# Second block, layer 0: seven half-size products for four projection pairs and three output pairs

## What is computed

```python
def second_block(x, c, ctx, c_ctx, w_mod, b_mod, ..., w_in, ..., w_out, ...):
    z = ctx
    for l in range(DEPTH):                                        # DEPTH = 2
        ...                                                       # first feed-forward part
        hx = modulate(rms_norm_2(x), mx[3], mx[4]) @ w_in[l]      # 1024 -> D_IN columns
        hz = modulate(rms_norm_2(z), mz[3], mz[4]) @ w_in[l]
        mix_x, mix_z = token_mixing(hx, hz, ...)                  # fourier, neighbourhood attention,
                                                                  # gated linear attention, grouped attention
        x = x + mx[5] * (mix_x @ w_out[l])                        # 1024 -> 1024
        ...                                                       # second feed-forward part
        if not last:
            z = z + mz[5] * (mix_z @ w_out[l])
```

## Time and profile before

| | us |
|---|---|
| median of 3 runs | 3211.98 |
| all runs | 3211.64, 3211.98, 3214.20 |
| the profiled execution | 3210.66 |
| its span in the trace | 3208.9 |
| projection stage, first plain tile (1708.03) to the product after it (1779.74) | 71.7 |
| output stage, end of the last transposes (1934.12) to the sums of the next norm (1984.36) | 50.2 |

### The profile page before, as it was taken

How to read it: one execution, slowest core, us unless ns; L and a number is a source line. 1 busy time by engine, 2 the same in 40 slices (tenths; PEclk the granted TensorE clock), 3 DMA queues, 4 the chain that set the end, 5 groups by cost and what they waited for, 6 DMA issues and landing times.

```text
span 3208.9 us, 45998 instructions
## 1 busy us (share of the span) xinstructions
PE 3165.5 (99%) x17760; PEld 2696.8 (84%) x17760; DVE 2046.9 (64%) x3824; ACT 770.5 (24%) x1786; POOL 123.7 (4%) x221
## 2 busy tenths in 40 slices
PE   8999999999999999999999989999999999999999
PEld 7888899988888999888885645888888888866999
DVE  6678668666785586786863773564445646356575
ACT  2121124221211242210114362211122111145221
POOL 0000000000000000100000000000000000001000
PEclk9999999999999999999999999999999999999999
DMA  6744675556446665564534122652325535232563
GB/s 192 190 112 150 218 217 159 170 159 158 114 155 203 171 173 166 151 189 136 174 130 118 35 51 73 170 184 79 102 72 162 185 119 156 87 106 54 145 176 128
DMA packets 587609, 456.26 MB, mean 142 GB/s; under 512 B 27792, under 2 KB 568880, under 8 KB 587008
## 3 DMA queue, kind: packets, MB, share of 16 engines
q1 hardware_dynamic: 564544, 373.65, 40.5%
q0 software_dynamic: 21376, 77.97, 7.7%
q10 hardware_dynamic: 1472, 1.68, 0.2%
HBM read 452.21 MB, written 1.05 MB: 141 GB/s over the span
## 4 chain that ended last, share of the span: by engine, by line
PE 94%; DVE 2%; ACT 1%; POOL 1%; issue 1%; DMA 1%; ACTq 0%; DVEq 0%; SPq 0%
PE psum L2552 53%; PE psum L2338 31%; PE psum L2345 3%; PE psum L2768 3%; PE psum L2744 1%; PE psum L2703 0%; ACT arena L1598 0%; PE psum L2641 0%; POOL hh L1360 0%; PE psum L2413 0%; DVE arena L1996 0%; POOL arena L1247 0%; PE psum L2579 0%; PE psum L2376 0%; PE psum L2562 0%
## 5 line engine op out<-in xcount | busy, mean ns | idle before, releaser
L2338 PE MATMUL psum<-hh,ring 128*128 128x256 f32 (+1 forms) x3584 | 855.5, 397 | 3.3 <-DVE hh L1841 3.0
L2338 PEld LDWEIGHTS psum<-hh,ring 128*128 128x128 f32 x3584 | 677.4, 191 | 153.5 <-issue 69.3
L2552 PE MATMUL psum<-arena 128*128 128x128 f32 (+1 forms) x4288 | 728.5, 327 | 2.8 <-ACT arena L1620 2.0
L2552 PEld LDWEIGHTS psum<-arena 128*128 128x128 f32 x4288 | 651.3, 191 | 59.0 <-issue 3.8
L1620 ACT ACTIVATE arena<-psum 128x256 f32<-128x256 f32 (+1 forms) x608 | 207.4, 341 | 1115.6 <-PE psum L2552 1113.7
L2552 PE MATMUL psum<-arena,ring 128*128 128x256 f32 (+1 forms) x2544 | 449.6, 329 | 2.4 <-ACT arena L1620 2.4
L2552 PEld LDWEIGHTS psum<-arena,ring 128*128 128x128 f32 x2544 | 393.8, 191 | 37.7 <-issue 3.7
L2552 PE MATMUL psum<-hh,ring 128*128 128x256 f32 (+1 forms) x1920 | 349.9, 335 | 3.8 <-ACT hh L1607 3.8
L2552 PEld LDWEIGHTS psum<-hh,ring 128*128 128x128 f32 x1920 | 302.1, 192 | 38.0 <-issue 5.9
L2552 PE MATMUL psum<-hh,arena 128*128 128x256 f32 (+1 forms) x1664 | 329.3, 341 | 0.0
L2105 DVE TENSOR_TENSOR arena<-arena 128x256 f32<-128x256 f32 (+1 forms) x168 | 61.1, 364 | 382.3 <-ACT arena L1620 380.3
(11 more groups left out here) (291 smaller groups left out, 2428.6 us busy)
## 6 DMA issues: line engine op xcount, KB each, us to landing
ring<-in_ffn_w SPq DMA_DIRECT2D x176, 512.0 KB, 5.2
ring<-in_w_in SPq DMA_DIRECT2D x54, 1024.0 KB, 5.3
ring<-in_w_up SPq DMA_DIRECT2D x88, 512.0 KB, 5.2
ring<-in_w_in SPq DMA_DIRECT2D x84, 512.0 KB, 5.3
mod_rows<-in_w_mod_rows POOLq DMA_DIRECT2D x72, 512.0 KB, 3.8
mod_rows<-in_w_mod_late_rows POOLq DMA_DIRECT2D x60, 512.0 KB, 4.7
ring<-in_ffn_w SPq DMA_DIRECT2D x16, 1536.0 KB, 6.6
ring<-in_ffn_w SPq DMA_DIRECT2D x16, 1280.0 KB, 5.8
```

Source lines behind the costliest of these rows:

```text
L2338: ins = mm(o[0:rows_, 0:T], w[:, k, c0:c0 + rows_], src[:, k, 0:T], start=(k == 0), stop=(k == kt - 1))
L2552: ins = mm(o, lhs[q][:, k, :], src[q][:, k, :], start=(q not in HALF_AFTER and not second and k == 0), stop=(k == n - 1), skip_group_check ...
```

## The change

In layer 0 of the second block only:

- **Projection.** `gate_in`, tile `np` 0 and the two gates stay plain and first. The eight other tiles become four pairs by seven products, in the order gq (gqa_q), naq (na_q), nak (na_k), glaqk (gla_q and gla_k). VectorE makes the activations' sums (`hsum2`, four instructions) and the weights' sums of each pair. ScalarE copies product 0 of a pair (`pair_copy`), then does the squares and the last copy of the pair before (`pair_out`), then the pair's other copies. `nss` and `nrot` of a pair stand one pair later.
- **Output.** `out_front` 2 is gone, tiles 0 and 1 stay plain, tiles 2 to 7 become three pairs by seven products. `hsum3` (six VectorE instructions) makes the sums of the mixed activations after the last `at_o`.
- Chunks are loaded in the new order: gk, gq, naq, nak, glaqk.

```diff
@@ plan_second
+    def seven(key, *ahead):
+        p.step("pair_copy", l, key)
+        for k in ahead:
+            p.step("pair_out", l, k)
+        p.half_part(("pair", l, PAIR, key), HALF_ORDER)
...
+    else:
+        p.step("hsum2", l)
+        p.step("wsum", l, PAIR, "pair", "gq")
+        project_plain(0)
+        gates()
+        p.step("wsum", l, PAIR, "pair", "naq")
+        seven("gq")
+        squared(0)
+        p.step("wsum", l, PAIR, "pair", "nak")
+        seven("naq", "gq")
+        squared(1)
+        squared(2)
+        turned(0)
+        p.step("wsum", l, PAIR, "pair", "glaqk")
+        seven("nak", "naq")
...
+        seven("glaqk", "nak")
+        squared(5)
+        squared(6)
+        turned(2)
+        p.step("pair_out", l, "glaqk")
...
-        if n == len(units) + 1:
+        if n == len(units) + 1 and last:
             out_front(2)
...
+        if not last and i == 0:
+            p.step("hsum3", l)
+        if not last and i in (0, 2, 4):
+            p.step("wsum", l, OUT, "pair", OUT_PAIRS[i // 2])
+        if not last and i // 2 in OUT_PAIRS:
+            if i % 2 == 0:
+                p.half_part(("pair", l, OUT, i // 2), HALF_ORDER)
+            continue
         p.step("out", l, i)
@@ ScalarE
+                elif kind == "pair_copy":
+                    name = ("pair", l, PAIR, r[0])
...
+                    produced(act, j)
+                    do(nc.scalar.activation(copy_of(name, 0), half_bank(name, 0), ACT.Copy), half_copied,
+                       4 * n + half_copies(name).index(0) + 1)
+                elif kind == "pair_out":
...
+                    evacuated(act, job[(*name, 5)])
...
+                        do(nc.scalar.activation(sqb2[:, 1, :], lead_of(name), ACT.Square), pair_squared, 2 * m + 1)
...
+                    free(nc.scalar.activation(val_of(name)[:, 0:S], bank(j)[:, 0:S], ACT.Copy), j)
...
+                        do(nc.scalar.activation(sqb2[:, 0, :], val_of(name), ACT.Square), pair_squared, 2 * m + 2)
@@ VectorE
+                elif kind == "hsum2":
...
+                    do(tt(p_t1, b12, b11, ALU.subtract))
...
+                    do(tt(p_t4, b21, p_t2, ALU.subtract), pair_summed, 1)
+                elif kind == "hsum3":
...
+                    for m in range(n_units // 2):
+                        evacuated(dve, job[("at_o", l, m)])
...
+                    do(tt(o_t4, mixt[:, 4:KT, 0:S], o_t2, ALU.subtract), pair_summed, 2)
@@ TensorE
+                        if kind == "pair" and q in (2, 4):
+                            pe.wait_ge(pair_summed, 1 + (w == OUT))
```

More of the change, by code:

```diff
@@ L55 @@
 HALF = S // 2
-FIRST = 2
+FIRST, PAIR, OUT = 2, 3, 4
+PAIR_KEYS = ("gq", "naq", "nak", "glaqk")
+OUT_PAIRS = (1, 2, 3)
 UP_SUMS = (3, 7, 11, 15, 19, 21)
@@ L552, in plan_second, with project_plain @@
     chunk_of = {6: "gk", 4: "gq", 5: "gq", 0: "naq", 1: "naq", 2: "nak", 3: "nak"}
-    for n in range(len(order) + 2):
-        if n < len(order):
-            p.step("np", l, n, order[n])
-            p.job("np", l, n, chunk=("w2", l, chunk_of[order[n]]))
-        if n == 0:
-            for d in range(2):
-                p.step("gate", l, d)
-                p.job("gate", l, d)
-            for i in range(2):
-                p.step("gp", l, i)
-                p.job("gp", l, i, chunk=("w2", l, "glaqk"))
-        if 1 <= n <= len(order):
-            p.step("nss", l, n - 1, order[n - 1])
-            p.job("nss", l, n - 1)
-        m = n - 3 if last else n - 2
-        if m >= 0 and order[m] >= 4:
-            p.step("nrot", l, m, order[m])
-            p.job("nrot", l, m)
+    def project_plain(n):
+        p.step("np", l, n, order[n])
+        p.job("np", l, n, chunk=("w2", l, chunk_of[order[n]]))
@@ new lines, in gates, with squared, turned @@
+    def gates():
+        for d in range(2):
+            p.step("gate", l, d)
+            p.job("gate", l, d)
+    def squared(n):
+        p.step("nss", l, n, order[n])
+        p.job("nss", l, n)
+    def turned(n):
+        p.step("nrot", l, n, order[n])
+        p.job("nrot", l, n)
+    def seven(key, *ahead):
[3 more added lines that the diff above has]
+        p.half_part(("pair", l, PAIR, key), HALF_ORDER)
+    if last:
+        for n in range(len(order) + 2):
+            if n < len(order):
+                project_plain(n)
+            if n == 0:
+                gates()
+                for i in range(2):
+                    p.step("gp", l, i)
+                    p.job("gp", l, i, chunk=("w2", l, "glaqk"))
+            if 1 <= n <= len(order):
+                squared(n - 1)
+            m = n - 3
+            if m >= 0 and order[m] >= 4:
+                turned(m)
+    else:
+        p.step("hsum2", l)
+        p.step("wsum", l, PAIR, "pair", "gq")
+        project_plain(0)
+        gates()
+        p.step("wsum", l, PAIR, "pair", "naq")
[8 more added lines that the diff above has]
+        seven("nak", "naq")
+        squared(3)
+        squared(4)
+        turned(1)
+        seven("glaqk", "nak")
[3 more added lines that the diff above has]
+        p.step("pair_out", l, "glaqk")
@@ L1060, in pieces @@
                 return hi - lo, 2 * P, src
-            elif kind == "w2":
+            elif kind == "pair" and name[2] == OUT:
+                src = [(rows(a["w_out_2"][l]), 256 * name[3], 256)]
+            elif kind in ("w2", "pair"):
                 w = rows(a["w_in_2"][l])
@@ L1365, in _ @@
                         pool.wait_ge(row_summed, COLUMN_STEPS)
[L1366 removed]
+                        produced(pool, job[("pair", 0, OUT, OUT_PAIRS[-1], PROD - 1)])
                     else:
@@ L1675, in _ @@
                     j = job[("gv", l, r[0])]
+                    if l < DEPTH - 1:
+                        evacuated(act, job[("pair", l, PAIR, "glaqk", 5)])
                     produced(act, j)
```

133 lines of the change are left out of this document (106 added, 27 removed).

## The result

The changed kernel takes **3218.0 us** (median; 3216.6 to 3218.8) against 3211.6 (3209.9 to 3214.2) for the kernel before: ratio 1.0020, interval 1.0013 to 1.0026. It is 6.4 us slower, inside the range that was forecast (3206 to 3218.5) and at its upper edge; the forecast was 3214.9. As a change the forecast was +2.9: it stood on a median of 3212.0 from three runs of the kernel before, and over 18 runs that median is 3211.6. The profiled execution has a span of 3215.6 us, 6.7 more than before.

A forecast was written before the change was run, and what follows sets the result against it. TensorE, busy for 99% of the span, was taken as the bound. Terms -0.4 + 2.0 + 0.0 - 0.4 + 1.7 = +2.9 us gave 3214.9 us, with an 8-in-10 range of 3206 to 3218.5.

The forecast's parts named there:

- The gross gain: Projection and output: a pair takes 12.09 us against 13.72 for two plain tiles, 11.4 us saved in all.
- rival 3: Projection: no wait behind the gates, first term -7.3 us and no first clock fall, 3206.0 us; chance 0.07.
- The wait behind the gates: Projection, pair gq: TensorE waits 6.9 us before product 2 for ScalarE's copy of product 0, queued behind both gates.
- rival 4: Projection and output: neither long wait occurs, -11.7 us in all, 3200.3 us; chance 0.05.
- The bank: Output: 1.1 us wait before the last at_o, 4.0 before pair 1 for tile 1's bank; stage 0.0 us in sum.
- The clock behind the two waits: Behind the projection's and the output's long wait: lowered TensorE clock costs 2.0 and 1.7 us.
- Rival 1: Both long waits occur, but the clock stays up at the second or at either, 3211.2 to 3213.2 us; chance 0.12.
- The rest of the projection: Projection after the first wait: every queue keeps up, naq's copy is in time, and the stage ends 0.4 us sooner.
- rival 5: Projection: gq's weights load late and delay the gate chain, +7.1 us, 3219.1 us; chance 0.08.
- hsum2: Projection: VectorE's four sums of 1.23 us follow complete h, end by 1713.1, nobody waits; nothing moves up to the gates.
- The tail: After the last output pair: VectorE has one addition instead of two, so the norm's sum comes 0.4 us sooner.
- clearly slower: Whole kernel: slower by more than 6.4 us, the measurement's bound for no change; chance 0.09.

The follow-up runs named there:

- all3: The changed kernel with three edits: first output pair in a free bank, gates' readouts behind the pairs, VectorE's first subtraction on h after h's last tile; 3198.9 us.
- gates: The changed kernel with ScalarE's and VectorE's readouts of both gates moved behind pairs gq and naq, TensorE's order kept; 3208.5 us.
- bank: The changed kernel with the first output pair begun one bank further on, in bank 2 instead of bank 1; 3212.1 us.
- after: The changed kernel itself, with both the projection and the output change, against the kernel before; 3218.0 us.
- hsum: The changed kernel with the first of VectorE's four subtractions on h waiting for the last tile of h instead of tile 3; 3216.7 us.
- out_only: The changed kernel with the projection stage of the kernel before put back, so only the output stage is changed; 3214.2 us.
- filler: The changed kernel with three projection pairs instead of four, the two GLA tiles plain again right behind the gates' products; 3216.7 us.
- delay2: The kernel before with only useless work added, the projection's last sum of squares repeated for 1.72 us more on TensorE; 3216.8 us.

## Why the prediction came out as it did, step by step

**The gross gain: right.** Pairs of 12.09 us, also in the output; all3 gives the projection 7.25 us (7.3 in rival 3's term).

**The wait behind the gates: right.** 6.80 for 6.9; mechanism shown by the run gates. Rivals 3 and 4 are false for this order of steps. All3 is rival 4's case made real, forecast at 3200.3, measured at 3198.9. The closeness is in part luck: in its trace the projection gained 7.25 us (7.3) and output and norm 3.92 (4.4), while the mixing lost 1.95 that the rival didn't have.

**The bank: right.** 1.16 before the last at_o (1.1), 3.87 before pair 1 (4.0). The run bank shows that the sums at product 2 are covered, with 1.65 us to spare (1951.40 for a start at 1953.05). The stage without its clock term is +0.3 where 0.0 was forecast, 0.2 of it because pair 1 starts that much later after the last transpose.

**The clock behind the two waits: right.** Forecast 2.0 and 1.7, in all 3.7, measured 1.64 and 1.76, in all 3.4: from start to start the 24 matmuls behind the first wait take 6.82 us in after and 5.18 in all3 (1720.85 to 1726.03), and the pair behind the second 13.85 for 12.09. Rival 1 (no fall at the second wait) is false in all five traces with that wait (after, gates, hsum, out_only, filler). The Trainium skill, page "TensorE: Matmul & The Clock Gate", section "Why this matters for your kernels", advises against idle gaps between bursts of matmuls; the runs bank and gates agree, for each fall left with its wait.

**The rest of the projection: right.** -0.4 and 2.0 were forecast from tile 0 on, +1.6; measured +1.22 (71.71 before, 72.93 after). The weights' sums of gq ended at 1714.63, so rival 5 is false, and naq's copy was in time. A table load of 1.28 us was again followed by its instruction 0.02 us later (1739.61 + 1.28, then 1740.91). The drain of about 1.38 us that the Trainium skill, page "ScalarE: Activation LUTs", section "What ACT_TABLE_LOAD costs", adds is not in these rows.

**hsum2: wrong.** "Nobody waits for it" was true, and its cost is not in a wait for it. It runs beside GpSimd's scalings and makes them longer, 5.80 for 4.73 us, and tile 0 stands behind those. The prediction had hsum2 wait for the whole of h; the kernel lets its first subtraction go once tile 3 is there, at 1706.48, and GpSimd's row ends at 1708.04. The failed step is the sentence that up to the gates nothing moves: +1.07 us.

**The tail: wrong by 0.34.** Squares and root did come sooner, but the gain is 0.06 us for 0.4. The norm's sum had moved to bank 7, the bank of the modulation, whose next matmuls then waited 0.75 us, mostly in place of the 0.72 us that TensorE waited for VectorE there before. With the bank out of the way (runs bank and all3) the gain is 0.2 us, so 0.15 of the miss is the bank, and the rest is that the term was sized too high. I had walked the banks for the pairs and not for what comes after them.

**What no step held: the mixing, +2.07.** The shift went through up to the wait (-0.30 there), and then a longer clock fall and a new one added 2.37. I took the clock term as a property of the two new waits; the earlier trace rows already had one stretch of 3.4 us at a wait in the mixing, and I didn't ask whether it would stay at 3.4. The other eleven traces have 6.8 at this wait, with and without the edits; why before has 3.4 is open.

**The sum.** Forecast +2.9, profiled +6.7: 1.07 from hsum2, 2.07 from the mixing, 0.34 from the tail, 0.3 from the output, less 0.4 from the clock behind the first wait, come to 3.4, and with 0.1 from the second clock term to 3.5 of the 3.8; 0.3 more arise behind the first feed-forward product (6.37 there, 6.7 at the end). The range held by 0.5 us, and that is luck: its upper part was meant for longer falls behind the two new waits, and what filled it were mostly losses that no step held. At a ratio of 1.0020 the result sits on the bound that was set for "no change". The chance of 0.09 for clearly slower was too small: the losses that I had listed all came at about their size, and those that I had not listed (1.07 and 2.07) came on top.

## What to carry to other kernels

When a step is split into products that hang on each other's copies, write down for each copying engine what already stands in its queue at that point, and put long chains that nobody waits for (here the gates) behind the first copies: three small edits turned +6.4 into about -11 us. Follow the banks and the neighbours of added work on to the next stage, not only to the end of the edit. Before an effect of some us is read as the edit's own, delay the old kernel by about as much and look whether the clock does the same, and take more than one trace of each kernel.

## What the runs showed of the hardware

- **Adding 1.7 us of work to a kernel cost 5 us.** Work of 1.72 us added to the kernel before raised its median by 5.05, and 2.58 us by 4.6. In the traces the granted clock is 0.5 for 6.8 us instead of 3.4 at the end of the same wait and behind it, and again near 1895 for 3.4 us, where the kernel before has no fall; these two make 2.40 us (delay2, mixing after the wait). In the ten traces of changed kernels and delays taken in the experiments, the second half of the mixing takes 73.74 or 73.78 us (out_only, gates, without the fall near 1890) or 74.24 to 74.83 (the others), and 72.25 only before. What decides whether and for how long the clock falls at such a place is left open; being later in time does not decide it alone.
- **VectorE slows GpSimd.** One f32 subtraction of 128x1024 on VectorE (1.23 us) beside GpSimd's scalings of 128x256 f32 made eight of them take 5.80 us instead of 4.73, about as much longer as it lasts itself. Its length was the 1.23 us that it has elsewhere: GpSimd paid, VectorE didn't.
